# The nine smallest experts of a mixture share three 128-row slots, side by side in the columns of TensorE's array

## The reference, cut to what matters

```python
glog = t @ w_rg + b_rg                       # 4 groups; the best one is taken
elog = (t @ w_re + b_re)[the chosen group]   # 4 experts in it; the best two are taken
combine = one_hot(expert_id) * (softmax(evals) * gval)
for e in range(16):
    he = silu(t @ w_gate[e]) * (t @ w_up[e])             # 1024 -> 512, twice
    y = y + combine[:, e:e + 1] * (he @ w_down[e])       # 512 -> 1024
return rms_norm_2(x + y, g_final)
```

## Time and profile before

| | |
|---|---|
| median of 3 runs | 2111.74 us (2111.05 to 2112.39) |
| the profiled execution | 2118.86 us, its span 2117.1 us |
| TensorE busy | 2051.1 us, 97% of the span |
| VectorE, ScalarE, GpSimd busy | 60%, 47%, 7% |
| HBM traffic | 339.17 MB, 160 GB/s over the span |
| the mixture's weight loads | 62 gate, 55 up and 64 down tiles into RAW; 11 more into ST and X |

### The profile page before, as it was taken

The page is one execution under the profiler, slowest core; times in us unless marked ns, Lnnn a source line. Parts: engine busy times, 40 slices in busy tenths (PEclk is TensorE's granted clock), DMA queues, the critical chain, the costliest instruction groups (busy, mean ns, idle before and its releaser), DMA issues.

```text
span 2117.1 us, 27859 instructions
## 1 busy us (share of the span) xinstructions
PE 2051.1 (97%) x10571; PEld 1612.4 (76%) x10571; DVE 1270.6 (60%) x2201; ACT 992.4 (47%) x1642; POOL 145.0 (7%) x246
## 2 busy tenths in 40 slices
PE   8999999999999999989999999999899999999997
PEld 7877778888888877758888888878678887645662
DVE  5575856585846356666756765737653556645563
ACT  4445545455534355544554563533562244244562
POOL 0000020000001000001000002102000000111111
PEclk9999999999999999989999999999999999999998
DMA  6235244642532333313425262452425426899997
GB/s 206 77 105 164 90 136 140 198 147 83 199 120 80 101 119 123 108 45 110 153 96 182 97 210 80 132 164 90 144 76 165 142 75 234 306 315 346 380 387 289
DMA packets 194428, 339.17 MB, mean 160 GB/s; under 512 B 15712, under 2 KB 103024, under 8 KB 194288
## 3 DMA queue, kind: packets, MB, share of 16 engines
q1 hardware_dynamic: 190096, 327.09, 45.5%
q0 software_dynamic: 4192, 10.23, 2.1%
HBM read 307.91 MB, written 31.72 MB: 160 GB/s over the span
## 4 chain that ended last, share of the span: by engine, by line
PE 81%; DVE 6%; DMA 6%; ACT 3%; POOL 2%; issue 2%; SPq 1%; DVEq 0%; ACTq 0%; POOLq 0%
PE ps L181 75%; PE ps L184 5%; DMA RAW<-in_w_down_dram 2%; POOL SM L216 1%; SPq L221 1%; DVE WL L196 1%; ACT ST L192 1%; DVE X L206 1%; POOL SM L213 1%; DMA ONDP<-qkd 1%; DMA ed<-ST 1%; ACT WH L192 0%; DMA NQ<-qqd 0%; DVE BR L196 0%; DVE JP L196 0%
## 5 line engine op out<-in xcount | busy, mean ns | idle before, releaser
L196 DVE TENSOR_TENSOR WL<-RAW,WH 128x1024 fp32r<-128x1024 f32 x388 | 469.3, 1223 | 257.0 <-ACT WH L192 253.8
L192 ACT ACTIVATE WH<-RAW 128x1024 fp32r<-128x1024 f32 x388 | 405.7, 1056 | 309.2 <-PE ps L181 184.3
L181 PE MATMUL ps<-XH,WH 128*128 128x512 f32 (+1 forms) x880 | 324.3, 369 | 3.8 <-DVE WL L196 3.8
L181 PE MATMUL ps<-XL,WH 128*128 128x512 f32 (+1 forms) x880 | 321.4, 365 | 0.0
L181 PE MATMUL ps<-XH,WL 128*128 128x512 f32 (+1 forms) x880 | 320.9, 365 | 0.0
L181 PE MATMUL ps<-WH,XH 128*128 128x512 f32 (+1 forms) x736 | 297.0, 404 | 2.1 <-ACT ST L192 2.1
L181 PE MATMUL ps<-WH,HR 128*128 128x512 f32 x928 | 289.3, 390 | 0.0
L181 PE MATMUL ps<-WH,XL 128*128 128x512 f32 (+1 forms) x736 | 285.0, 387 | 0.0
L181 PE MATMUL ps<-WL,XH 128*128 128x512 f32 (+1 forms) x736 | 284.2, 386 | 0.0
L181 PEld LDWEIGHTS ps<-WH,HR 128*128 128x128 f32 x928 | 174.2, 188 | 36.0
L181 PEld LDWEIGHTS ps<-XH,WH 128*128 128x128 f32 x880 | 168.6, 192 | 30.2 <-DVE WL L196 4.6
(11 more groups left out here) (362 smaller groups left out, 2917.9 us busy)
## 6 DMA issues: line engine op xcount, KB each, us to landing
RAW<-in_ffn_w_dram SPq DMA_DIRECT2D x164, 512.0 KB, 4.7
RAW<-in_w_down_dram SPq DMA_DIRECT2D x64, 512.0 KB, 15.3
RAW<-in_w_gate_dram SPq DMA_DIRECT2D x62, 512.0 KB, 13.1
RAW<-in_w_up_dram SPq DMA_DIRECT2D x55, 512.0 KB, 14.3
RAW<-in_w_in_dram SPq DMA_DIRECT2D x30, 512.0 KB, 4.5
RAW<-in_ev_w_in_dram SPq DMA_DIRECT2D x20, 512.0 KB, 4.5
RAW<-in_ple_w_gate_dram SPq DMA_DIRECT2D x16, 512.0 KB, 3.8
RAW<-in_od_w_in_dram SPq DMA_DIRECT2D x32, 256.0 KB, 3.6
```

The lines of the kernel that those rows point to most:

```text
L181: return self.go(ns).matmul(o, lhsT=l, rhs=x, start=st, stop=sp)
L192: return self.go(0.83 * n + 55.0 + (130.0 if bias is not None else 0.0) + (100.0 if acc is not None else 0.0)).activation(o, i, f, scale=s ...
L196: return self.go(1.04 * n + 68.0).tensor_tensor(o, a, b, op)
```

## The change

The nine small slots become three slots of 128 rows, numbered 0 to 2, in which several experts lie side by side: places 0 and 1 with 64 rows each; places 2 to 5 with 32 each; places 6, 7 and 8 with 32, 32 and 64. Large slots are 3 to 9, the second slots of the two largest are 10 and 11. There are 12 slots in place of 18, and 11 possible steps behind them in place of 8. In a shared slot each expert's rows are the stationary operand for its own columns of the array and its own rows of the output; gate and up now have a bank each (`fan_shared`), and `fold_shared` does the same for the down product. The group order is new, the last slot added on chip is slot 2, and a shared slot is scattered once for each of its experts, each time with a list that names only that expert's rows. Since the experts alternate from tile to tile in a shared slot, SyncE reads OVF before each of its loads.

```diff
-    GROUPS = ((0,), (1,), (15, 17), (2,), (14, 16), (3,), (13,), (4,), (12,), (5,), (11,), (6,), (10,), (9,), (7,), (8,))
+    SHARED = {0: ((0, 0, 64), (1, 64, 64)), 1: ((2, 0, 32), (3, 32, 32), (4, 64, 32), (5, 96, 32)),
+              2: ((6, 0, 32), (7, 32, 32), (8, 64, 64))}
+    GROUPS = ((0,), (1,), (7,), (6,), (8, 10), (5,), (9, 11), (4,), (3,), (2,))
-    LAST = SLOTS[-2:]
+    LAST = SLOTS[-1]
...
-            for n, gr in enumerate(GROUPS):
+            yield from fan(GROUPS[0])
+            yield from fold(GROUPS[0])
+            yield from fan(GROUPS[1])
+            for n, gr in enumerate(GROUPS[2:]):
                 yield from fan(gr)
-                if n:
-                    yield from fold(GROUPS[n - 1])
+                yield from fold(GROUPS[n + 1])
             yield from fold(GROUPS[-1])
...
+        def fan_shared(i):
+            for k in range(0, 8, 2):
+                tiles = [[weight(p, name, k, "whole")[0] for p, _, _ in SHARED[i]] for name in ("w_gate_2", "w_up_2")]
+                for g in range(2):
+                    pe.wait_ge(*(yield [("ex", i, k // 4), *[("raw", c) for c in tiles[g]],
+                                        G.ask(("fan", i, g)) if k == 0 else None]))
+                    ex, o = pe.slot("ex", i)[1], pe.slot("fan", i, g)
+                    for h in range(2):
+                        for c, (p, r, n) in zip(tiles[g], SHARED[i]):
+                            t = pe.mm(o[r:r + n, :], ex[:, k + h, r:r + n], whole_tile(c)[:, h, :], k + h == 0, k + h == 7,
+                                      856 / len(SHARED[i]))
...
+        def fold_shared(i):
+            for k in range(4):
+                tiles = [weight(p, "w_down_2", k, "whole")[0] for p, _, _ in SHARED[i]]
+                for nh in range(2):
+                    for c, (p, r, n) in zip(tiles, SHARED[i]):
+                        t = pe.mm(o[r:r + n, :], eh[:, k, r:r + n], whole_tile(c)[:, nh, :], k == 0, k == 3,
+                                  856 / len(SHARED[i]))
...
         def spread_last():
-            for i, T in [(i, T) for t in ((0, 1), (2,), (3,)) for i in LAST for T in t]:
+            for T in range(4):
                 for h in range(2):
-                    t = pe.mm(pe.slot("sp", 0, h, T)[:, :], SELF[LAST.index(i)][p, cols(T)], pe.slot("y", i)[0][p, 0:512],
-                              i == LAST[0], i == LAST[1], 445)
+                    t = pe.mm(pe.slot("sp", 0, h, T)[:, :], SELF[:, cols(T)],
+                              pe.slot("y", LAST)[0][:, h * 512:h * 512 + 512], True, True, 856)
...
-            v.tt(R8[:, :, 0:64], iota[:, 0:64].unsqueeze(1).broadcast_to([128, 8, 64]),
+            v.tt(R8.rearrange("p b (s c) -> p b s c", s=2), iota[:, 0:64].unsqueeze(1).unsqueeze(1).broadcast_to([128, 8, 2, 64]),
...
-            v.ts(b64, place, 8.5, 64.0, ALU.is_gt, ALU.mult, 16).then_inc(*v.sig("dve_vec"))
-            v.ts(s64, place, 13.5, 64.0, ALU.is_gt, ALU.mult, 16).then_inc(*v.sig("dve_vec", d.new()))
-            v.ts(cap1, b64, 64.0, None, ALU.add, None, 16).then_inc(*v.sig("dve_vec"))
-            v.stt(cap2, b64, 64.0, s64, ALU.add, ALU.add, 16).then_inc(*v.sig("dve_vec", d.new()))
+            v.ts(a5, place[:, q], 5.5, None, ALU.is_gt, None, 14).then_inc(*v.sig("dve_vec"))
+            v.ts(a7, place[:, q], 7.5, 32.0, ALU.is_gt, ALU.mult, 14).then_inc(*v.sig("dve_vec"))
...
+            v.stt(off[:, q], u1, -2.0, b9, ALU.add, ALU.mult, 14).then_inc(*v.sig("dve_vec"))
+            v.stt(slot[:, q], u2, 1.0, a5, ALU.add, ALU.add, 14).then_inc(*v.sig("dve_vec"))
...
         def scatters():
-            for i in SLOTS[:-2]:
+            for i in SLOTS[:-1]:
+                lists = [PUT[:, i:i + 1]] if i not in SHARED else [PUT[:, 12 + p:13 + p] for p, _, _ in SHARED[i]]
+                for m, at in enumerate(lists):
+                    g.wait_ge(*(yield [*last]))
+                    last = [("sum", i, m)]
...
         def back():
-                s.wait_ge(*(yield [("sum", SLOTS[-3]), XROWS[T]]))
+                s.wait_ge(*(yield [("sum", SLOTS[-2]), XROWS[T]]))
```

More of the change, by code:

```diff
@@ L354, in build @@
     C0, D0 = 132, 138.5
+    STEPS, SL = 11, 24
     def zone(name, off, shape, dt=F32):
@@ L801, in fan @@
                             t.then_inc(*pe.sig("pe_gemm", *keys))
+        def fan_shared(i):
[9 more added lines that the diff above has]
+                                      856 / len(SHARED[i]))
+                            end = k + h == 7 and (p, r, n) == SHARED[i][-1]
+                            keys = ([("wf", c)] if h else []) + ([("fan", i, g)] if end else []) + (
+                                [("free", ("ex", i))] if end and g else [])
+                            if keys:
+                                t.then_inc(*pe.sig("pe_gemm", *keys))
         def fold(gr):
+            if gr[0] in SHARED:
+                yield from fold_shared(gr[0])
+                return
             for k in range(4):
-                c, wh, wl = weight(gr, "w_down_2", k)
+                c, wh, wl = split_weight(gr, "w_down_2", k)
                 for i in gr:
@@ L1565, in hidden @@
             for i in slots:
-                if not small(i):
+                if not small(i) and i not in SHARED:
                     yield [("esT", i, 0)]
@@ L1602, in count @@
         def count():
-            a.wait_ge(*(yield [("ovf",), ("fan", 4)]))
-            a.over = a.e.value_load(OVF[0:1, 0:1], min_val=0, max_val=8)
+            a.wait_ge(*(yield [("ovf",), ("fan", 5, 0)]))
+            a.over = a.e.value_load(OVF[0:1, 0:1], min_val=0, max_val=STEPS)
         def final(T):
@@ L2683, in pool @@
             (2, zeros()), (4, gathers(SLOTS)), (2, scatters()), (8, count()),
-        ], lambda j: [(4, gathers([18 + j]))], [(2 + T, final(T)) for T in range(4)]
+        ], lambda j: [(4, gathers([12 + j]))], [(2 + T, final(T)) for T in range(4)]
     def sync(s):
@@ L2857, in count @@
         def count():
-            s.wait_ge(*(yield [("ovf",), ("fan", 4)]))
-            s.over = s.e.value_load(OVF[0:1, 0:1], min_val=0, max_val=8)
+            s.wait_ge(*(yield [("ovf",), ("fan", 5, 0)]))
+            s.over = s.e.value_load(OVF[0:1, 0:1], min_val=0, max_val=STEPS)
         def final(T):
@@ L2973, in build @@
     OVERC = len(TILES)
-    for j in range(8):
+    for j in range(STEPS):
         lister.through(extra(j)[0][1])
```

285 lines of the change are left out of this document (164 added, 121 removed), and 4 rows, old and new, of the table scored.

## The result

Before 2111.74 us (2110.6 to 2115.0), changed 2131.24 us (2124.54 to 2133.79), five runs each: ratio 1.0084, 95% interval 1.0063 to 1.0104. Forecast was 2098 (2087 to 2107). The profiled execution of the changed kernel took 2127.3 us, its span is 2125.5.

The account below looks back on a forecast made before the run. The weight-tile stream was taken to set the end, TensorE mattering where held buffers stop it. Last tile 12.7 us earlier plus 1.4 us at the end, 14.1 us off 2111.74, gave 2098 us, range 2087 to 2107.

Parts of the forecast that it names:

- Tiles ahead of the router: Before the sorted experts' tiles: 24 tiles loadable early instead of 20, four fitting a hole; gain 5.1 us.
- router: Before the sorted tiles: a larger first comparison and added small operations make OVF later; cost to the stream 1.6 us.
- reads of OVF: SyncE's 84 loads in slots 1 and 2, a read each: mostly hidden by the stream; 0 to 6 us, taken as 1.
- idle at the start: Stream from 1816 to 1920: slots 0 and 1 free tiles faster, leaving 3 of 11 us idle; gain 8 us.
- TensorE, the price of a group: Shared slots: strips run side by side at 0.86 to 0.89 us a group, 21 us a slot; TensorE loses some 46 us.
- The fourth rival: Slots 1 and 2: strips of 32 columns do not run side by side; 2151 us; chance 0.08 together with the fifth.
- The large slots in a row: After slot 1: TensorE needs 113.5 us, the stream reaches its buffer limit; may lose 0 to 6 us, taken as 1.
- The third rival: Behind the stream: waiting scatters delay X by 8 us, or a low clock costs 6; 2103 to 2107; chance 0.15.
- The end: Behind the last tile: last groups, spread matmuls and what follows take 22.2 us instead of 23.6.
- the 2 us for the low clock: At the end: after waits TensorE's clock is halved, adding some 2 us for the last group and first spread matmuls.
- the prediction's own signs of being wrong: Share below 1.0 from 1850 to 1900 or near 2030; `X<-sum` after the last tile; fours over 1.3 us; further-step instructions.
- The scatters' bytes: Scatters of the mixture: 6.03 MB become 5.24 MB, 0.8 MB less at 4.1 us a MB; gain 3.3 us.

Follow-up runs that it names:

- e1: The changed kernel with slot 2's 64-row expert multiplied as two strips of 32 columns from the same weight tile; 2110.32 us, ratio 0.9983 to before.
- e2: The changed kernel with slot 2's fan reordered to 32, 32, 32, 32, 64, 64 for two groups; 2127.85 us, one run.
- e3: e1 with slot 0 mixed too (64, 32, 32) while slot 2 keeps equal strips; 2132.27 us, ratio 1.0090 to before.
- e14: e5 with shared slots' scatters cut to fewer rows and 20 weight buffers instead of 24 behind tile 27; 2124.53 us, ratio 1.0064 to before.
- e5: e1 with four buffers `EY` instead of three; 2105.83 us, ratio 0.9950 to before.
- e15: e1 without the product of the weights' low part in the large slots and with four `EY`; 2104.10 us, ratio 0.9957 to before.
- e13: e5 with shared slots' scatters cut to fewer rows and 28 weight buffers instead of 24 for the first 168 tiles; 2110.36 us, ratio 0.9984.

## Why the prediction was wrong, point by point

- **Tiles ahead of the router, router, reads of OVF, idle at the start**: right. Four tiles early; 1.5 us for the router (1.6 forecast); share 1.03 from 1820 to 1970, so nothing of slot 1's 48 reads shows, and 1.03 again from 2050 to 2080, where slot 2's last ones are read; 1.02 for 0.93 in 1816 to 1920.
- **TensorE, the price of a group: the step that failed.** I took one price for all shared slots, with "as the pair, 0.86 to 0.89 us a group" below and four in series above. Fours of 32 meet the lower end (0.88) and pairs too. Slot 2's three strips are not of one width, and lie between: 1.99. I had both ends and put the mixed slot at the lower one without asking what is new in it. The fourth rival has the right mechanism with the wrong place: the strips of slot 1 do run side by side, those of unequal width do not. e1, e2 and e3 show it: 21 us (16 by the stage) of the 33 between 2098 and 2131. The Trainium skill, "TensorE: Matmul & The Clock Gate", measured speedup, gives 2.38 for three column strips, from which I had estimated 1.08 us. No run here has three strips of one width; four take 0.86 to 0.88 and the mixed three 1.99.
- **The large slots in a row: mis-sized.** "May lose 0 to 6 us; I take 1": it is 12 (share 0.87 over 80 us, in the changed kernel as in e1). My sum of TensorE's work from `fan` 6 to `fold` (9, 11) was 113.5 us; the changed kernel took 121.5 (1914.2 to 2035.7), with gaps of 4.1, 4.6 and 2.6 us between large matmuls. In part these are transposes, in part waits for VectorE's `EX` and for ScalarE's evacuation into `EY` (the 3.47 us shown above). And the limit is steep: e14. That the large slots' stretch costs the 12 us is read from the share; no single edit gave them back in the old order.
- **The third rival's chain of scatters**: seen, earlier than I placed it. I let it end at `X<-sum`; in the changed kernel that goes out at 2098.89 and holds nobody. It acts through `EY` on ScalarE, and from there on the conversions. The buffers `EY` stood in none of my terms.
- **The end**: right in number, by luck in part. In e1, from the last tile's matmuls at 2087.33 to 2109.0, 21.7 us; forecast 22.2. But the 2 us for the low clock did not come (it reads 1.00 from 2087 to 2096, after a wait of 0.71 only), and X was not back in time: `X<-sum` goes out at 2089.60, behind the last tile, and VectorE waits for it:

```profile
2093.10 2.59 DVE L198 TENSOR_TENSOR X<-ps,X 128x512 f32<-128x512 f32 x4 [16.30 <-DMA X<-sum]
...
2096.59 2.58 DVE L198 TENSOR_TENSOR X<-ps,X 128x512 f32<-128x512 f32 x4 [0.90 <-DMA X<-sum]
```

  TensorE's last matmul ends at 2096.36 and the last addition at 2099.17, some 2 us later than one addition of 0.7 us behind it would. That is one of the prediction's own signs of being wrong, and its 2 us stand by chance where the clock's 2 us stood. In e5 it is the other way round: X is in time, and after the wait of 4.25 us the clock reads 0.57 from 2086 to 2090 and the two groups take 3.46 us for 1.92.
- **The scatters' bytes** fell by 1.27 MB (10.23 to 8.96; 0.8 forecast); what that gave in time no run separates.
- **The sum, redone for e1**: from the first sorted tile to the last one 264.2 us were forecast, 2087.3 - 1812.2 = 275.1 came, 11 more. That is what the large slots took above my 1 us (12 for 1); it is a difference of two sums, not measured by itself.

What stays open: why the stream still falls back in the large slots of e5 and e15, where TensorE's work and the chain count little; how much of each difference comes from the new order that `lay_out` gives with each edit, which no run holds fixed; and whether e13 fell short by GpSimd's order alone.

## What to carry to other kernels

When work is packed side by side in the array, make all parts of a group the same width, even if one tile is then read twice: the extra matmul is free, the odd width costs a whole pass. A bound taken from a pair of equal parts holds for equal parts only. Where work is taken off an engine at its limit, list the buffers that tie the other engines to each other in that stretch: here 26 us less of TensorE gained nothing with three `EY`, and with a fourth the same kernel was 11 us faster. And read the busy time again after such a cut: an engine that waits more at a lower clock gives back less than the sum of its instructions.
